# The triangular inverse of a recurrent chunk: four of its five levels in 32x32 tiles on the diagonal, the fifth as one joining block

## The reference

```python
def rwkv7_step(state, inp):
    r_t, w_t, k_t, v_t, kk_t, ka_t = inp
    sa = jnp.einsum('bhvk,bhk->bhv', state, -kk_t)
    state = (state * w_t[:, :, None, :] + sa[..., None] * ka_t[:, :, None, :]
             + v_t[..., None] * k_t[:, :, None, :])
    return state, jnp.einsum('bhvk,bhk->bhv', state, r_t)
```

## Time and profile before

| | |
|---|---|
| runs | 1580.79, 1582.12, 1583.65 us |
| span of the profiled execution | 1580.2 us (the profile gives no other time of this execution) |
| PE busy | 1536.4 us (97%) |
| DVE, ACT, POOL busy | 871.6 (55%), 697.8 (44%), 118.5 (8%) us |
| chunk loop | 192 to 396 us |
| chunks 5, 6, 7 | some 22.9 us each |

### The profile page before, as it was taken

One profiled execution on the slowest core, in us unless ns is written; L12 is line 12 of the kernel. 1 busy time (PEld: TensorE's weight loads), 2 busy tenths in 40 slices (PEclk: granted clock), 3 DMA queues, 4 the chain that ended last, 5 costly groups with the idle time before them and its releaser, 6 DMA issues.

```text
span 1580.2 us, 38947 instructions
## 1 busy us (share of the span) xinstructions
PE 1536.4 (97%) x16258; PEld 1446.1 (92%) x16258; DVE 871.6 (55%) x1487; ACT 697.8 (44%) x1120; POOL 118.5 (8%) x257
## 2 busy tenths in 40 slices
PE   8999999999999999999999999999899999999998
PEld 7999899899699999999999999965599999999886
DVE  5578743443555666666333445366556666766222
ACT  5555233333545444444222588367635444443121
POOL 1450293300000000000000000000000000000000
PEclk9999999999999999999999999999999999999999
DMA  5222000000123332333333232330023333233331
GB/s 155 68 67 81 22 4 4 4 4 4 38 74 93 93 92 83 91 93 95 96 88 85 66 93 80 87 119 1 1 81 94 93 93 92 86 88 115 95 91 72
DMA packets 210748, 113.65 MB, mean 72 GB/s; under 512 B 8032, under 2 KB 207410, under 8 KB 210642
## 3 DMA queue, kind: packets, MB, share of 16 engines
q1 hardware_dynamic: 210034, 109.93, 24.0%
q10 hardware_dynamic: 608, 2.16, 0.4%
HBM read 109.95 MB, written 2.13 MB: 71 GB/s over the span
## 4 chain that ended last, share of the span: by engine, by line
PE 90%; ACT 4%; DVE 3%; issue 2%; SPq 1%; DMA 0%; DVEq 0%; ACTq 0%
PE BK L667 88%; PE BK L1192 2%; ACT XB L1250 1%; ACT PTT L1250 1%; SPq L397 0%; DVE MQA L1758 0%; ACT L1250 0%; DVE U L2224 0%; DVE WLO L1758 0%; ACT ALL L1250 0%; ACT WHI L1250 0%; PE BK L1126 0%; ACT PR L1250 0%; DMA PRAW<-in_ffn_conv_b_dram 0%; DVE XB L1758 0%
## 5 line engine op out<-in xcount | busy, mean ns | idle before, releaser
L1758 DVE TENSOR_TENSOR WLO<-RAW,WHI 128x1024 fp32r<-128x1024 f32 (+1 forms) x182 | 236.3, 1298 | 135.9 <-ACT WHI L1250 134.9
L1250 ACT ACTIVATE WHI<-RAW 128x1024 fp32r<-128x1024 f32 (+1 forms) x182 | 203.0, 1115 | 223.7 <-PE BK L667 223.4
L667 PE MATMUL BK<-YNH,WLO 128*128 128x264 f32 (+1 forms) x1216 | 248.0, 286 | 0.0
L667 PE MATMUL BK<-YNH,WHI 128*128 128x264 f32 (+1 forms) x1216 | 247.6, 285 | 0.0
L667 PE MATMUL BK<-YNL,WHI 128*128 128x264 f32 (+1 forms) x1216 | 246.8, 284 | 0.0
L667 PE MATMUL BK<-XNH,WHI 128*128 128x258 f32 (+1 forms) x1056 | 216.4, 286 | 2.6 <-DVE PB L1758 2.0
L667 PE MATMUL BK<-XNH,WLO 128*128 128x258 f32 (+1 forms) x1056 | 213.4, 284 | 0.0
L667 PE MATMUL BK<-XNL,WHI 128*128 128x258 f32 (+1 forms) x1056 | 213.0, 283 | 0.0
L667 PEld LDWEIGHTS BK<-YNH,WHI 128*128 128x128 f32 x1216 | 190.0, 189 | 0.5 <-issue 0.3
L667 PEld LDWEIGHTS BK<-YNH,WLO 128*128 128x128 f32 x1216 | 188.9, 189 | 0.0
L667 PEld LDWEIGHTS BK<-YNL,WHI 128*128 128x128 f32 x1216 | 188.3, 189 | 0.0
(11 more groups left out here) (297 smaller groups left out, 2219.8 us busy)
## 6 DMA issues: line engine op xcount, KB each, us to landing
RAW<-in_ffn_w_up_dram SPq DMA_DIRECT2D x88, 512.0 KB, 3.8
RAW<-in_ffn_w_down_dram SPq DMA_DIRECT2D x32, 704.0 KB, 4.7
RAW<-in_odd_w_in_dram SPq DMA_DIRECT2D x24, 512.0 KB, 3.9
RAW<-in_even_w_in_dram SPq DMA_DIRECT2D x22, 512.0 KB, 3.9
CB<-cum_dram SPq DMA_DIRECT2D x8, 528.0 KB, 8.3
RAW<-in_even_w_out_dram SPq DMA_DIRECT2D x8, 512.0 KB, 4.0
RAW<-in_odd_w_out_dram SPq DMA_DIRECT2D x8, 512.0 KB, 4.2
XIN<-in_x_dram ACTq DMA_DIRECT2D x4, 512.0 KB, 5.9
```

Source lines behind the costliest of these rows:

```text
L667: return pe.matmul(o, l, r, start=start, stop=stop, skip_group_check=check)
L1250: return nc.scalar.activation(o, i, f, **kw)
L1758: return nc.vector.tensor_tensor(o, x, y, op)
```

## The change

The matrices A and X are block diagonal in 32x32 blocks as long as the blocks joined are no larger than 32, which holds up to level 3. The changed kernel therefore computes only the two 32x32 diagonal blocks of each head at levels 0 to 3 and in `transposed`: four matmuls of 32x32 by 32 for a pair, each in its own tile on the array's diagonal (`BLOCKS`), instead of two of 64x64 by 64. The blocks beside the diagonal are zero; bank 3 + 2g is cleared once ahead of the loop, so that ACT can still copy whole 64x64 matrices.

At level 4 only the joining block is formed: one 32x32 product per head for the residue, a DVE copy of 96 columns in place of the masked product, and one 32x32 product per head in `corrected`, written to 96 further columns of bank 2 + 2g. A new DVE step, `joined`, subtracts it into X in SBUF. ACT has no copy at level 4 any more. `solved` of the chunk waits for `joined` (semaphore `x_done`) where it waited for ACT.

```diff
+BLOCKS = [(slice(32 * j, 32 * j + 32), slice(32 * (j % 2), 32 * (j % 2) + 32)) for j in range(4)]
+HEAD_BLOCKS = [(slice(64 * e, 64 * e + 32), slice(64 * e + 32, 64 * e + 64)) for e in range(2)]
+LOW, HIGH = slice(0, 32), slice(32, 64)
...
                     for q in range(G3):
-                        for h in HEADS:
-                            x = mm(BK[h, 3 + 2 * g, C * q:C * q + C], XB[h, c % 2, g, 1, q, :], IDENT[h, h])
+                        for b, d in BLOCKS:
+                            x = mm(BK[b, 3 + 2 * g, C * q + d.start:C * q + d.stop], XB[b, c % 2, g, 1, q, d], IDENT[b, b])
...
                 def residue(c, n, g):
 
-                    pe.wait_ge(S(f"x_up{g}"), (LEVELS + 1) * c + n + 1)
+                    pe.wait_ge(S(f"x_up{g}"), LEVELS * c + n + 1)
+                    if c and n == 0:
+                        pe.wait_ge(S(f"x_done{g}"), c)
                     for q in range(G3):
                         p = G3 * g + q
-                        for h in HEADS:
-                            x = mm(BK[h, 2 + 2 * g, C * q:C * q + C], AT[h, c % 2, p, :], XB[h, c % 2, g, 0, q, :])
+                        if n == LEVELS - 1:
+                            for lo, hi in HEAD_BLOCKS:
+                                x = mm(BK[hi, 2 + 2 * g, 32 * q:32 * q + 32], AT[lo, c % 2, p, HIGH],
+                                       XB[lo, c % 2, g, 0, q, LOW])
+                            continue
+                        for b, d in BLOCKS:
+                            x = mm(BK[b, 2 + 2 * g, C * q + d.start:C * q + d.stop], AT[b, c % 2, p, d],
+                                   XB[b, c % 2, g, 0, q, d])
...
-                def corrected(c, n, g, last):
+                def corrected(c, n, g, short):
 
                     pe.wait_ge(S(f"t_mask{g}"), LEVELS * c + n + 1)
-                    if not last:
+                    if n == LEVELS - 1:
                         for q in range(G3):
-                            p = G3 * g + q
-                            for h in HEADS:
-                                mm(BK[h, 3 + 2 * g, C * q:C * q + C], XB[h, c % 2, g, 1, q, :], TM[h, p, :])
+                            for lo, hi in HEAD_BLOCKS:
+                                x = mm(BK[lo, 2 + 2 * g, 6 * C + 32 * q:6 * C + 32 * q + 32], TM[hi, G3 * g + q, LOW],
+                                       XB[hi, c % 2, g, 1, q, HIGH])
+                        x.then_inc(S(f"x_mm{g}"), 1)
+                        return
...
+                        for b, d in BLOCKS:
+                            x = mm(BK[b, 3 + 2 * g, C * (G3 + q) + d.start:C * (G3 + q) + d.stop], TM[b, G3 * g + q, d],
+                                   XB[b, c % 2, g, 1, q, d])
...
+                ve.wait_ge(S("s5_ucp"), 4)
+                ve.wait_ge(S("bonus"), PAIRS)
+                ve.memset(BK[:, 3:6:2, 0:6 * C], 0.0).then_inc(S("off_blocks"), 1)
...
+                ve.memset(BK[:, 2:5:2, 6 * C:6 * C + 32 * G3], 0.0).then_inc(S("off_blocks"), 1)
...
+                def joined(c, g):
+
+                    ve.wait_ge(S(f"x_mm{g}"), (LEVELS + 1) * (c + 1))
+                    x = XB[:, c % 2, g, 1, :, HIGH]
+                    tt(x, x, BK[:, 2 + 2 * g, 6 * C:6 * C + 32 * G3].rearrange("p (q t) -> p q t", t=32), ALU.subtract)\
+                        .then_inc(S(f"x_done{g}"), 1)
```

More of the change, by code:

```diff
@@ L553, in _ @@
                 od.settle()
-                for n in range(LEVELS):
+                for n in range(LEVELS - 1):
                     b = 2 << n
@@ L893, in residue @@
                     x.then_inc(S(f"t_mm{g}"), 1)
-                def corrected(c, n, g, last):
+                def corrected(c, n, g, short):
                     pe.wait_ge(S(f"t_mask{g}"), LEVELS * c + n + 1)
-                    if not last:
+                    if n == LEVELS - 1:
                         for q in range(G3):
-                            p = G3 * g + q
-                            for h in HEADS:
-                                mm(BK[h, 3 + 2 * g, C * q:C * q + C], XB[h, c % 2, g, 1, q, :], TM[h, p, :])
+                            for lo, hi in HEAD_BLOCKS:
[3 more added lines that the diff above has]
+                        return
+                    if not (short and n == SHORT_LEVELS - 1):
+                        for q in range(G3):
+                            for b, d in BLOCKS:
+                                mm(BK[b, 3 + 2 * g, C * q + d.start:C * q + d.stop], XB[b, c % 2, g, 1, q, d],
+                                   TM[b, G3 * g + q, d])
@@ L903, in corrected @@
                     for q in range(G3):
-                        p = G3 * g + q
-                        for h in HEADS:
-                            x = mm(BK[h, 3 + 2 * g, C * (G3 + q):C * (G3 + q) + C], TM[h, p, :], XB[h, c % 2, g, 1, q, :])
+                        for b, d in BLOCKS:
+                            x = mm(BK[b, 3 + 2 * g, C * (G3 + q) + d.start:C * (G3 + q) + d.stop], TM[b, G3 * g + q, d],
+                                   XB[b, c % 2, g, 1, q, d])
                     x.then_inc(S(f"x_mm{g}"), 1)
@@ L926, in removed, with solved @@
                         x.then_inc(S(f"rec_mm{g}"), 1)
-                def solved(c, levels):
+                def solved(c, short):
                     for g in range(2):
                         pe.wait_ge(S(f"rec_cp{g}"), 3 * c + 1)
-                        pe.wait_ge(S(f"x_up{g}"), (LEVELS + 1) * c + levels + 1)
+                        if short:
+                            pe.wait_ge(S(f"x_up{g}"), LEVELS * c + SHORT_LEVELS + 1)
+                        else:
+                            pe.wait_ge(S(f"x_done{g}"), c + 1)
                         for q in range(G3):
@@ L989, in _ @@
                             if n == 0:
-                                solved(c - 1, LEVELS)
+                                solved(c - 1, False)
                             elif n < 3:
@@ L997, in _ @@
                         for g in range(2):
-                            corrected(c, n, g, n == levels - 1)
+                            corrected(c, n, g, short)
                     if not short:
@@ L1004, in _ @@
                         transposed(c + 1, 1)
-                solved(CHUNKS - 1, SHORT_LEVELS)
+                solved(CHUNKS - 1, True)
                 for g in range(2):
@@ L1570, in _ @@
                             taken(c + 1, p)
-                        for g in range(2):
-                            corrected(c, n, g, n == levels - 1)
+                        if n < LEVELS - 1:
+                            for g in range(2):
+                                corrected(c, n, g, n == levels - 1)
                     if not short:
@@ L2216, in _ @@
                     if not short:
+                        for g in range(2):
+                            joined(c, g)
                         products(c + 1, PAIRS - 1)
```

14 lines of the change are left out of this document (10 added, 4 removed).

## The result

The changed kernel takes 1631.25 us (median of 4 runs, 1629.72 to 1634.81), the kernel before 1581.45 us beside it (4 runs, 1579.92 to 1583.65). The ratio is 1.0317, 95% interval 1.0305 to 1.0330: 50 us slower, where the prediction had 11 us less and a range up to 1594. The profiled executions agree, 1630.6 us after and 1580.2 before.

What follows compares the result with a forecast made beforehand. TensorE was taken to bound the loop. Shorter steps less shape changes and longer waits gave 12.1 us less over all chunks, less 0.7 at the entry: 11.4 us less, 1570.7 us, range 1556 to 1594.

Steps and rivals of the forecast that it cites:

- the record rate binds: TensorE's queue, 226 steps: above about 48 ns a round slower, 1588 or about 1660 us; 41 to 60 ns 0.22, longer 0.13.
- Term A: Shorter steps on TensorE's array: 258 steps of 0.204 us in place of 0.351, 37.9 us less.
- Term B: TensorE's changes between 64x64 and 32x32 tiles wait for the array to empty: 0.256 us a pair, 58 pairs, 14.8 us.
- drains free: Rival: changes between 32x32 and 64x64 tiles cost nothing; 24 us less, 1558 us; chance 0.10.
- Term C: TensorE's waits, mainly for ACT's copies of X, grow as shorter steps cover less: 1.34 us a chunk.
- The entry: Two clears on DVE ahead of the first MQA, 0.95 and 0.36 us, delay the path by 0.7 us once.
- The clock: Rival: waits at every level bring 1.2 GHz for a fifth of the loop; 26 us slower, 1608 us; chance 0.05.
- three signs of being wrong: 24-record row over 0.5 us; another shape's loads starting while the last record streams; clock under 1 in an undisturbed chunk.

Runs made afterwards that it cites:

- join_alone: The changed kernel with levels 0 to 3 and transposed back in 64x64 tiles, leaving only level 4's joining block; 1582.04 us, ratio 1.0008 to the kernel before.
- whole_one_pass: The kernel before, all in 64x64 tiles, with the inverse's products on upper halves as bf16, one record in place of two; 1552.63 us, ratio 0.9821.
- one_pass: The changed kernel with its 32x32 products on upper halves as bf16, one record in place of two; 1563.33 us, ratio 0.9882 to the kernel before.
- corrected3_and_join: join_alone with corrected of level 3 in 32x32 tiles too; 1580.72 us, ratio 0.9994 to the kernel before.
- one_pass_twice: one_pass with every single-record 32x32 product issued twice in a row; 1631.44 us, ratio 1.0314 to the kernel before.
- levels01_and_join: The changed kernel with levels 2 and 3 and transposed back in 64x64 tiles, levels 0, 1 and 4 small; 1597.11 us, ratio 1.0113 to the kernel before.
- two_junctions: corrected3_and_join with corrected of level 0 and the residue of level 1 in 32x32 tiles too; 1590.08 us, ratio 1.0050 to the kernel before.

## Why the prediction was wrong, point by point

**What failed: the sum had no term for the supply of instructions.** The step is the sum's list of costs: the shorter steps, the shape changes, the waits for copies and the entry. It put the price of the additional instructions, 24 records a step in place of 12, at nothing beyond the time between two records. In its place the loop waited 36 us on issue, its 65 blocks 3.86 us each, and took 251 us; measured 1631.25 us where the sum had 1570.7. Queue 8 stood on the page of the kernel before with 84 packets, and the prediction never divided 2712 new records by 128. It would have found 21 blocks more. It also would have found no price for a block, because before none had made TensorE wait (0.2 us on issue in the loop). The nearest bound was in the trace: the packets lay no closer than 3.57 us even in dense stretches, and a middle of 64x64 work uses a block up in 3.75 us. The rival "the record rate binds" was the right place, TensorE's supply of work, with the wrong mechanism. It asked how fast one record follows another, and that was fast, 8 to 9 ns. The limit lies in how fast 128 of them follow the last 128. That the time fell between the rival's two prices, 1588 at 13 ns a record and 1660 at 29, was luck.

**Term A, right where the instructions were there.** A mean round of 35 ns, predicted 34; 24 records in 0.39 us, predicted 0.4.

**Term B, right in mechanism and about right in size.** The timeline after, at level 4 of a chunk:

```profile
362.42 0.38 PE L670 MATMUL BK<-XB,AT 32*32 32x32 f32 x12 [0.50 <-ACT XB L1272]
362.73 0.65 PE L670 MATMUL BK<-ALL 64*64 64x128 f32 x8
...
362.73 0.41 PEld L670 LDWEIGHTS BK<-ALL 64*64 64x64 f32 x8
```

The records of 32x32 end at 362.80 and the 64x64 tile's weights load at 362.73, 0.07 us ahead, as in the earlier trace rows. A record lasts 0.191 us, predicted 0.193. The prediction's own terms add up to 0.12 and 0.144 us, 0.264 a pair and not 0.256, which is 0.5 us over the loop. join_alone came out within 1 us of its sum, and whole_one_pass 10.7 us below one_pass where the 58 pairs were priced at 14.8. Both fit the size; neither measures it alone. The rival "drains free" falls by the 0.07 us, which it denied.

**Term C.** TensorE's loads waited 16.8 us for ACT's XB, predicted some 22, before 11.8. The pauses on issue gave the copies time, so this number does not test the term. In corrected3_and_join, where such pauses are 1.5 us, the shorter `corrected` of level 3 raised this wait by 1.2 us over join_alone's, PE's own by 1.5; the term had 2.6 for it. The direction is as the term said, the size smaller.

**The entry, right in mechanism, half its size.** DVE's first MQA starts at 187.32 us, 0.4 us later than before where 0.7 was predicted; the clears took 0.70 and 0.22 us, estimated at 0.95 and 0.36:

```profile
185.74 0.70 DVE L2180 MEMSET BK<- 128x768 f32 x1 [0.30 <-DVE ALL L1781]
...
187.20 0.22 DVE L2190 MEMSET BK<- 128x192 f32 x1
```

**The clock.** The rival gave it 0.05 and a fifth of the loop at 1.2 GHz; it was a quarter, 65 of 251 us. So of the prediction's three signs of being wrong the third appeared, a clock under 1 in a chunk (0.94), and the other two did not at the full clock. The accounts: busy time should have fallen by the 37.9 of term A to 152.8 us, and is 198.0. Up to 15 of these 45 us are shape changes, and about 29 are the half of the 58 us in which TensorE was busy at the low clock. Idle time rose by 42, of it 36 on issue. Taken one by one these suggest that clock and supply share the loss.

The distances of the packets bound the clock's share. In the changed kernel they average 3.71 us at the full clock (37 of them), 3.89 mostly at the low one (12), and 3.84 over the loop, those that lie in both included. If all 65 came at 3.71 the loop would be 241 us, so by this estimate some 10 of the 49 us are the clock's and the others are the supply's. In one_pass_twice the two averages are equal. What would happen to the clock if the supply were faster was not tried. one_pass at 0.91 suggests that it would still cost something wherever TensorE waits for ACT.

**What stays open.** It is open which part of the 3.6 to 4.3 us is the packet's way (the packets themselves took 0.9 to 1.5 us), which is the engine taking the block over, and why the next packet starts only 1.0 to 1.6 us after TensorE goes on. No run separated these. Nor is it shown what brings the low clock: it follows a wait of 3 us at the earlier trace rows, a pause of 1.3 us at 350 and one of 1.9 us at 374, but what decides it no run told apart.

## What to carry to other kernels

When a change makes TensorE's instructions smaller and more, count them in blocks: divide the records by 128 (an fp32 call is two records, each with its weight load), take the distance of the instruction queue's packets from the trace, and compare it with the time in which the array uses a block up. In none of the eleven traces do two packets in the loop lie closer than 3.23 us, and where the supply bound the median was 3.7 us, 29 ns a record on average over some hundred records. Pairs of 64x64 fp32 tiles were already there (29 ns). Three finer cuts in fp32 lost (the changed kernel, levels01_and_join, two_junctions); the two with the fewest additional small records (join_alone, corrected3_and_join) were level with before. A single pass in place of two helped by 29 us on the array (whole_one_pass), and in the changed kernel it ended the shortage as well (one_pass), if its precision can be borne.

## What the runs showed of the hardware that was not expected

- TensorE ran 24 records of 32x32 in four tiles at 8.8 ns a record (0.21 us a step). The Trainium skill (TensorE: Matmul & The Clock Gate, "Wait — 56ns, not 53.3ns?") has no distance between starts below about 25 ns. The trace disagrees for records that go to four different tiles in turn. What held the kernel back was the coming of whole blocks.
- At the full clock a record's time in its own tile followed the wider of its weights and its moving operand, each record with its own weight load. With weights of 64 columns it is 58.5 ns for 64 moving columns and 54 to 57 ns for 32 (two tiles run side by side, hence 29 and 27 to 29 ns a record). With weights of 128 columns it is 112 ns at 64 moving columns, as at 128. With 32 and 32 it is 32 to 35 ns, and with weights of 32 columns and 132 moving columns 112.
- A wait on issue inside a step, with no semaphore there, ended 2.2 to 2.9 us after the start of a packet on the instruction queue, in all 34 cases over 0.5 us of the changed kernel's loop.
- In one_pass_twice blocks came 3.85 us apart at the full clock and 3.86 at the low one.
